# One moving operand of 512 columns, its high half and its low half side by side, in the feed-forward stages and in the expert U loop

## The reference, cut to what matters

```
def peer(xn, w_q, sub_keys, u_tab, v_tab):      # per token: 8 heads x 16 chosen of 16384 experts
    ...
        act = gelu(einsum("phkd,pd->phk", u_tab[ib], tb))
        return einsum("phk,phkd->pd", gb * act, v_tab[ib])

feed-forward, for each of D_FF = 2816 features, 2 layers:
    gate, up = split(x @ w_in)                  # 1024 -> 2 x 2816
    hidden   = silu(causal_conv3(gate) + bias) * up
    y        = hidden @ w_out                   # 2816 -> 1024
```

## Time and profile before

| | |
|---|---|
| median of 3 runs | 1781.97 us |
| the profiled execution's own time | 1776.27 us |
| its span, first to last instruction | 1774.4 us |
| PE (TensorE) busy | 1686.2 us, 95% |
| DVE (VectorE) busy | 1237.4 us, 70% |
| ACT (ScalarE) busy | 902.1 us, 51% |
| granted TensorE clock, mean | 0.978 |
| moved by DMA | 292.43 MB, mean 165 GB/s |

### The profile page before, as it was taken

How to read it: one execution, slowest core, us unless ns; L and a number is a source line. 1 busy time by engine, 2 the same in 40 slices (tenths; PEclk the granted TensorE clock), 3 DMA queues, 4 the chain that set the end, 5 groups by cost and what they waited for, 6 DMA issues and landing times.

```text
span 1774.4 us, 30819 instructions
## 1 busy us (share of the span) xinstructions
PE 1686.2 (95%) x11158; PEld 1543.3 (87%) x11158; DVE 1237.4 (70%) x2305; ACT 902.1 (51%) x1530; POOL 106.6 (6%) x92
## 2 busy tenths in 40 slices
PE   7999799999999999999999998988999989889997
PEld 7999699889999999999988887767999878679997
DVE  7888769979995555555556665666766776466666
ACT  5666632168874444444444454544444445444443
POOL 0000000035540000000000000000000000000000
PEclk9999999999999999999999999989999989889999
DMA  6556634513345555565656665324556544245552
GB/s 206 172 179 215 222 107 149 184 60 109 118 135 198 187 183 187 188 188 183 187 187 193 195 225 180 117 83 143 189 182 187 188 143 130 85 154 180 187 189 96
DMA packets 83290, 292.43 MB, mean 165 GB/s; under 512 B 11152, under 2 KB 12944, under 8 KB 82832
## 3 DMA queue, kind: packets, MB, share of 16 engines
q1 hardware_dynamic: 81568, 286.00, 49.8%
q10 hardware_dynamic: 1648, 5.45, 0.9%
HBM read 289.31 MB, written 2.10 MB: 164 GB/s over the span
## 4 chain that ended last, share of the span: by engine, by line
PE 87%; issue 7%; DVE 3%; ACT 2%; POOL 0%; DMA 0%; SPq 0%; DVEq 0%; ACTq 0%; POOLq 0%
PE ps L1040 16%; PE ps L1041 15%; PE ps L1042 15%; PE ps L1059 10%; PE ps L1061 10%; PE ps L1063 10%; PE ps L1124 5%; PE ps L1148 3%; PE ps L1035 1%; ACT high L670 1%; DVE h_tok L1413 1%; DVE low L1346 1%; DVE xl L1367 0%; DMA subln<-in_subln 0%; PE ps L1112 0%
## 5 line engine op out<-in xcount | busy, mean ns | idle before, releaser
L1346 DVE TENSOR_TENSOR low<-raw,high 128x1024 fp32r<-128x1024 f32 (+1 forms) x517 | 622.3, 1211 | 345.9 <-ACT high L670 332.5
L670 ACT ACTIVATE high<-raw 128x1024 fp32r<-128x1024 f32 (+1 forms) x517 | 540.8, 1048 | 512.2 <-PE ps L1042 283.1
L1040 PE MATMUL ps<-xh,low 128*128 128x256 f32 x2376 | 683.2, 288 | 12.9 <-DVE xl L1367 6.8
L1041 PE MATMUL ps<-xl,high 128*128 128x256 f32 x2376 | 674.8, 284 | 0.0
L1042 PE MATMUL ps<-xh,high 128*128 128x256 f32 x2376 | 674.7, 284 | 0.0
L1040 PEld LDWEIGHTS ps<-xh,low 128*128 128x128 f32 x2376 | 458.1, 193 | 23.1 <-DVE xl L1367 7.5
L1041 PEld LDWEIGHTS ps<-xl,high 128*128 128x128 f32 x2376 | 458.4, 193 | 6.0 <-issue 1.7
L1042 PEld LDWEIGHTS ps<-xh,high 128*128 128x128 f32 x2376 | 458.0, 193 | 0.0
L1059 PE MATMUL ps<-high,yl 128*128 128x512 f32 x688 | 213.7, 392 | 0.1
L1061 PE MATMUL ps<-low,yh 128*128 128x512 f32 x688 | 212.7, 390 | 0.0
L1063 PE MATMUL ps<-high,yh 128*128 128x512 f32 x688 | 212.3, 390 | 0.0
(11 more groups left out here) (243 smaller groups left out, 1495.9 us busy)
## 6 DMA issues: line engine op xcount, KB each, us to landing
raw<-in_v_tab SPq DMA_DIRECT2D x128, 512.0 KB, 3.5
raw<-in_u_tab SPq DMA_DIRECT2D x104, 512.0 KB, 3.5
raw<-in_ffn_in SPq DMA_DIRECT2D x88, 512.0 KB, 3.5
raw<-in_w_mix SPq DMA_DIRECT2D x56, 512.0 KB, 4.2
raw<-in_ffn_out SPq DMA_DIRECT2D x44, 512.0 KB, 3.5
arena<-in_u_tab SPq DMA_DIRECT2D x24, 512.0 KB, 3.6
raw<-in_w_query SPq DMA_DIRECT2D x16, 512.0 KB, 5.7
raw<-in_diff_qk SPq DMA_DIRECT2D x16, 512.0 KB, 3.6
```

Source lines behind the costliest of these rows:

```text
L670: a.activation(cols(high, p, 0, n), cols(raw, p, 0, n), ACT.Copy).then_inc(slot_high[p.slot], 1)
L1040: pe.matmul(dst, left[1], right[0], start=start, stop=False)
L1041: pe.matmul(dst, left[0], right[1], start=False, stop=False)
L1346: v.tensor_tensor(cols(low, p, 0, n), cols(raw, p, 0, n), cols(high, p, 0, n).bitcast(F32), ALU.subtract).then_inc(slot_low[p.slot], 1)
```

## The change

`xh` and `xl` become the two halves of one tensor, `x_parts`. A new `project_in_halves` replaces `project_in` for the expert U pieces of the U loop and for gate and up. Per 128 x 128 block it issues one matmul with the high weights and 512 moving columns (the high chunk and the low chunk) and one with the low weights and 256 columns. The bank then holds two partial results, which have to be added. In the U loop VectorE adds them (`sum_halves`, a `tensor_reduce`) into `u_sum`, and GELU reads that. In the feed-forward stages ScalarE copies one half out of PSUM and VectorE adds the other to it.

```diff
+            def project_in_halves(p, b):
+                pe.wait_ge(slot_low[p.slot], p.count)
+                both = x_parts[:, :].rearrange("p (h k t) -> p h k t", h=2, k=KC)
+                for k in range(KC):
+                    pe.matmul(bank(b).rearrange("p (h t) -> p h t", h=2), cols(high, p, k * PARTS, PARTS), both[:, :, k, :],
+                              start=(k == 0), stop=False)
+                    ins = pe.matmul(bank(b, 0, SEQ), cols(low, p, k * PARTS, PARTS), chunk_of(xh, k), start=False, stop=(k == KC - 1))
+                ins.then_inc(slot_done[p.slot], 1)
# ScalarE, U loop
             def gelu_block(j, it=0, first=False):
-                p = piece_u(j, it)
-                a.wait_ge(slot_done[p.slot], p.count)
+                a.wait_ge(u_summed, it * 4 + (j + 1))
                 if not first:
                     a.wait_ge(coef_low, it * 4 + (j - 1))
-                a.activation(coef[j % 2], bank(4 + j % 4, 0, SEQ), ACT.Gelu_apprx_tanh).then_inc(gelu_ready, 1)
+                a.activation(coef[j % 2], u_sum[j % 2], ACT.Gelu_apprx_tanh).then_inc(gelu_ready, 1)
# TensorE, U loop: the bank is free once it is summed
-                        pe.wait_ge(gelu_ready, it * 4 + j)
-                    project_in(piece_u(j + 3, it), bank(4 + (j + 3) % 4, 0, SEQ))
+                        pe.wait_ge(u_summed, it * 4 + j)
+                    project_in_halves(piece_u(j + 3, it), 4 + (j + 3) % 4)
# VectorE, U loop (halves(b) is the bank as p t h)
+            def sum_halves(j, it=0, first=False):
+                p = piece_u(j, it)
+                v.wait_ge(slot_done[p.slot], p.count)
+                if not first:
+                    v.wait_ge(gelu_ready, it * 4 + (j - 1))
+                v.tensor_reduce(u_sum[j % 2], halves(4 + j % 4), AX.X, ALU.add).then_inc(u_summed, 1)
             def expert_step(j, it):
                 if j + 2 < LATE:
-                    weigh(j + 2, it)
+                    sum_halves(j + 2, it)
                 if j < LATE - 2:
                     ahead(piece_v(j, it))
+                if j + 2 < LATE:
+                    weigh(j + 2, it)
                 if j + 2 < NKEYS:
                     coef_low_part(j + 2, it)
...
# ScalarE, feed-forward
                 def hidden(n, it=0, first=False):
+                    e = n % 2
+                    a.wait_ge(slot_done[piece_gate(l, n, it).slot], piece_gate(l, n, it).count)
+                    a.activation(gate_sum[e], bank(4 + 2 * e, SEQ, SEQ), ACT.Copy).then_inc(s["gate_half"], 1)
                     ahead(piece_gate(l, n, it))
                     a.wait_ge(s["conv_ready"], it * 4 + (n + 1))
                     a.activation(act[n % 2], conv[n % 2], ACT.Silu).then_inc(s["silu_ready"], 1)
+                    a.wait_ge(slot_done[piece_up(l, n, it).slot], piece_up(l, n, it).count)
+                    a.activation(up_sum[e], bank(5 + 2 * e, SEQ, SEQ), ACT.Copy).then_inc(s["up_half"], 1)
                     ahead(piece_up(l, n, it))
...
# VectorE, feed-forward
-                    link(v.tensor_copy(p, at(ffn_params, it * 16 + (l * FF_CHUNKS + n) * 4, 4)))
-                    v.wait_ge(slot_done[piece_gate(l, n, it).slot], piece_gate(l, n, it).count)
+                    v.tensor_copy(p, at(ffn_params, it * 16 + (l * FF_CHUNKS + n) * 4, 4))
+                    v.wait_ge(s["gate_half"], it * 4 + (n + 1))
+                    link(v.tensor_tensor(gate, gate, bank(4 + 2 * e, 0, SEQ), ALU.add))
...
+                    v.wait_ge(s["up_half"], it * 4 + (n + 1))
+                    link(v.tensor_tensor(up, up, bank(5 + 2 * e, 0, SEQ), ALU.add))
                     v.wait_ge(s["silu_ready"], it * 4 + (n + 1))
-                    v.wait_ge(slot_done[piece_up(l, n, it).slot], piece_up(l, n, it).count)
-                    v.tensor_tensor(hid[e], act[e], bank(5 + 2 * e, 0, SEQ), ALU.mult).then_inc(s["hid_ready"], 1)
+                    v.tensor_tensor(hid[e], act[e], up, ALU.mult).then_inc(s["hid_ready"], 1)
```

More of the change, by code:

```diff
@@ L220, in build @@
         h_tok = sb("h_tok", [PARTS, TB * D])
-        xh = sb("xh", [PARTS, KC * SEQ], F32R)
-        xl = sb("xl", [PARTS, KC * SEQ], F32R)
+        x_parts = sb("x_parts", [PARTS, 2 * KC * SEQ], F32R)
+        xh, xl = x_parts[:, 0:KC * SEQ], x_parts[:, KC * SEQ:]
         yh = sb("yh", [PARTS, 2 * SEQ], F32R)
@@ L245, in bank, with halves @@
             return ps[:, b * HALF + lo:b * HALF + lo + n]
+        def halves(b):
+            return bank(b).rearrange("p (h t) -> p t h", h=2)
         def cols(t, p, lo=0, n=D):
@@ L295, in build @@
         coef = [h_tok[:, SEQ * n:SEQ * n + SEQ] for n in range(2)]
+        u_sum = [h_tok[:, 512 + SEQ * n:512 + SEQ * n + SEQ] for n in range(2)]
         weight = spare[:, :]
@@ L359, in build @@
         fpst = [part(1536 + 4 * n, 4) for n in range(2)]
+        gate_sum = [part(1600 + 256 * n, 256) for n in range(2)]
+        up_sum = [part(2112 + 256 * n, 256) for n in range(2)]
         fbias = stats[:, 44:45]
@@ L410, in build @@
         staged_ready, staged_weighed = sem("staged_ready"), sem("staged_weighed")
-        gelu_ready, coef_ready = sem("gelu_ready"), sem("coef_ready")
+        u_summed, gelu_ready, coef_ready = sem("u_summed"), sem("gelu_ready"), sem("coef_ready")
         xf_ready, early_done, early_gelu, early_weighed = (
@@ L426, in build @@
         fz_ready, fexp_ready, bias_ready = (sem(n) for n in ("fz_ready", "fexp_ready", "bias_ready"))
-        ffn_sems = [{n: sem(f"ffn{l}_{n}") for n in ("conv_ready", "silu_ready", "hid_ready", "hid_high", "hid_low")} for l in range(2)]
+        ffn_sems = [{n: sem(f"ffn{l}_{n}") for n in ("gate_half", "up_half", "conv_ready", "silu_ready", "hid_ready", "hid_high", "hid_low")} for l in range(2)]
         block = ctx.enter_context(nc.Block())
@@ L1159, in _ @@
                 pe.wait_ge(staged_weighed, STAGED - LEAD - 3 + j)
-                project_in(piece_u(j), bank(4 + j, 0, SEQ))
+                project_in_halves(piece_u(j), 4 + j)
             def expert_step(j, it):
@@ L1315, in gate_and_up @@
                 def gate_and_up(n, it=0):
-                    project_in(piece_gate(l, n, it), bank(4 + 2 * (n % 2), 0, SEQ))
-                    project_in(piece_up(l, n, it), bank(5 + 2 * (n % 2), 0, SEQ))
+                    project_in_halves(piece_gate(l, n, it), 4 + 2 * (n % 2))
+                    project_in_halves(piece_up(l, n, it), 5 + 2 * (n % 2))
                 def step(n, it):
@@ L1729, in expert_step @@
                     ahead(piece_u(j + 3, it))
+            sum_halves(0, first=True)
+            sum_halves(1, first=True)
             weigh(0)
@@ L1931, in hidden @@
                     e = n % 2
-                    gate = bank(4 + 2 * e, 0, SEQ)
+                    gate, up = gate_sum[e], up_sum[e]
                     p = fpst[e]
-                    link(v.tensor_copy(p, at(ffn_params, it * 16 + (l * FF_CHUNKS + n) * 4, 4)))
-                    v.wait_ge(slot_done[piece_gate(l, n, it).slot], piece_gate(l, n, it).count)
+                    v.tensor_copy(p, at(ffn_params, it * 16 + (l * FF_CHUNKS + n) * 4, 4))
+                    v.wait_ge(s["gate_half"], it * 4 + (n + 1))
+                    link(v.tensor_tensor(gate, gate, bank(4 + 2 * e, 0, SEQ), ALU.add))
                     link(v.tensor_scalar(conv[e], gate, p[:, 2:3], p[:, 3:4], ALU.mult, ALU.add))
@@ L1957, in ffn @@
                 hidden(0)
-                ffn_steps(v, step, chain, 3)
+                ffn_steps(v, step, chain, 4)
             attention("diff", att_sems[0], 3)
```

## The result

The changed kernel takes 1820.99 us (median of 4 runs, 1819.88 to 1824.0), the kernel before 1782.02 us in the same runs. The ratio is 1.022, 95% interval 1.0203 to 1.0238: 39 us slower. The profiled execution took 1821.72 us with a span of 1819.9 us. It stands beside the 1774.4 us span of before.

A forecast was written before the change was run, and what follows sets the result against it. PE was taken to bound the kernel before, and a closed VectorE-ScalarE circle the changed U loop. 45.4 us lost there less 7.3 gained in feed-forward gave 38.1 more: 1814.4 against the profiled execution, 1820 as median, range 1800 to 1840.

The forecast's parts named there:

- The circle: U loop: eight waits between VectorE and ScalarE close on themselves, 6.29 us per step against PE's 5.53; loop 45.4 us longer.
- The one link without a row: U loop, VectorE's sum out of PSUM: taken as 0.684 us, bounds 0.42 and 1.37.
- rival 2: U loop: the reduction is slow on PSUM read with a stride, 1.37 us, total 1865 us; chance 0.07.
- hand-over: U loop, from VectorE's sum to GELU on ScalarE: adds 0.03 us to the reduction, link 0.71.
- PE's pause per step: U loop: PE waits for `coef_low` some 0.75 us in each step once the lead is used up.
- Rival 1: PE's pace decides everywhere, the U-loop circle being under 5.53 us: 13.6 us gained, total 1768 us; chance 0.08.
- Rival 3: U loop: PE's new idle time lowers its granted clock, +78 us, total 1898 us; chance 0.03.
- The feed-forward term: Both feed-forward stages: 88 pieces at 0.092 us save 8.1 us, net of waits 7.3 us.
- the block on TensorE: PE, each 128 x 128 block: 0.359 us falls to 0.346 to 0.349, a saving taken as 0.0115 us.
- waits at the end: Last feed-forward step: PE waits 0.4 us more for the low part of the hidden block, 0.8 for both layers.
- A feed-forward step: Feed-forward stages: PE's step falls from 8.49 to 8.31 us, with PE busy throughout.
- the additions and copies are hidden: Feed-forward stages: PE's 8.31 us step covers VectorE's 6.7 and ScalarE's 4.6 us; uncovered they would cost 72 us.

The follow-up runs named there:

- e1: Changed kernel with one VectorE line moved: in each U-loop step weigh stands ahead of `low` of V, directly behind the sum; 1774.1 us, ratio 0.9959.
- e3: Changed kernel with the U-loop sum taken over 128 of the 256 tokens only, GELU reading these sums twice; 1805.13 us, ratio 1.0129.
- e4: Changed kernel with four more matmuls of 256 columns in each U piece of the U loop; 1821.27 us, ratio 1.0224.
- e6: Changed kernel with the sum of block j+3 placed at the end of VectorE's step j, weigh left behind `low` of V; 1775.64 us, ratio 0.9964.
- e7: e1 with each piece's eight 512-column matmuls first, then its eight of 256, where they alternated; 1764.49 us, ratio 0.9904.

## Why the prediction was right

**The circle.** Its sum, 6.29 us, came out to the hundredth, and the hundredth is luck: GELU of block 2 started at 541.48 and that of block 67 at 950.43, (950.43 - 541.48) / 65 = 6.29. Link by link, against rows 4 to 6, in the step shown above: `high` to `low` 1.07 and 1.08 (forecast 1.09), `low` to the next 1.14 and 1.14, sum to GELU 0.80 (0.71), GELU to `high` V 0.32 (0.33), weigh to `coef_high` 0.45, `coef_high` to `high` U 0.32. The one link without a row, the reduction, took 0.684 us, what the row with as many inputs had the earlier trace rows. Strided reading out of PSUM added nothing, and rival 2 (1.37 us) is out. What I mis-sized is its hand-over, 0.12 us in this step and not 0.03. In the next step the sum starts at 710.71 and GELU at 711.43, 0.72 later, a hand-over of 0.04. Over the 68 steps the two values are about equally common, and GELU comes 6.25 or 6.33 us after the one before it. The mean of this link is 0.755, 0.045 over the forecast; the other seven links together are 5.52 in the step shown, 0.06 under the forecast 5.58. The two errors all but cancel. The loop cost +45.6 between the landmarks, forecast 45.4. PE's pause per step was forecast at 0.76 us; it came to 0.65 to 0.70, since its own step is 5.59 us (as in e1: 705.84 - 700.25) and not 5.53, and inside a longer circle that costs nothing. e1, e3, e4 and e6 show the mechanism itself: reordered it goes, a shorter link shortens it one for one, and more PE work does nothing to the time.

**Rival 1** (PE's pace decides) had its turning point at 5.53 us of circle. It did not come true here. But in e1 and e6, whose circles are below that, PE's pace decides. The gain that this rival named, 13.6 us, is not reached there: the medians lie 8 and 5 us under those of before. e7, with the same matmuls in another order, gains 16.

**Rival 3** (the clock) is out: the granted clock stayed 1.00 in the loop with PE busy 185 of 200 us.

**The feed-forward term was mis-sized.** The step that failed is the block on TensorE: 0.347 us, put together from a spacing of 512 columns among 512s and of 256 among 256s. The rows of the changed kernel give, over ten blocks:

```profile
1281.16 0.39 PE L1068 MATMUL ps<-x_parts,high 128*128 128x512 f32 x1
...
1284.68 0.40 PE L1068 MATMUL ps<-x_parts,high 128*128 128x512 f32 x1
```

3.52 / 10 = 0.352, a saving of 0.007 us per block and not 0.0115, or 0.054 us per piece. Over 88 pieces that is 4.8 us; the landmarks give 4.9, the forecast was 8.1 less 0.8 of waits at the end, 7.3. Those waits were smaller too: in the last step of the first layer the starts of PE's rows on either side of the wait lie 0.89 us apart (1462.13 and 1463.02) where they lay 0.68 apart (1413.23 and 1413.91), 0.2 more and not 0.4, and in the second layer there is no such gap in either kernel. A feed-forward step was to take 8.31 us and takes 8.38:

```profile
1692.32 0.39 ACT L998 ACTIVATE arena<-ps 128x256 f32<-128x256 f32 x1 [1.69 <-PE ps L1070]
...
1700.70 0.39 ACT L998 ACTIVATE arena<-ps 128x256 f32<-128x256 f32 x1 [1.75 <-PE ps L1070]
```

e7 shows that the forecast 0.347 is there to be had, in another order. In the second feed-forward stage the first and the last start of the convolution lay 175.7 us apart before (L1936, 1580.2 to 1755.9); it is 173.2 in the changed kernel (L1969, 1629.0 to 1802.2) and 171.8 in e7 (L1969, 1574.5 to 1746.3). That is 3.9 us less per stage in e7, close to half of the forecast 8.1. In e1 the alternation took nearly all of the gain in the U loop: from first to last GELU 371.1 us (533.7 to 904.8) against 372.0 before (528.8 to 900.8). Part of it is that there the V piece also took 2.78 us instead of 2.75 (703.03 - 700.25). In e7 it takes 2.75 again (705.91 - 703.16), and the same stretch takes 365.9 us (533.4 to 899.3). Why the V piece is slower in the U loop of e1 is open. Its alternating neighbours alone don't do it: in the feed-forward stage of the changed kernel, between the same alternating matmuls, an out piece takes 1697.69 - 1694.95 = 2.74 us.

**That the additions and copies are hidden** in the feed-forward stages held: PE busy 150 of 150 us, VectorE 116.90 / 150 x 8.38 = 6.5 us per step (forecast 6.7).

The mis-sized gain is 2.4 us. With it put right, the forecast would have been 1822.4. That the measured time, 1821.0, lies only 1 us from the forecast 1820 is in part luck, within the scatter of the runs.

## What to carry to other kernels

When two engines work through fixed orders and hand work to each other, write down the circle that the orders close and add it up from start to start. A busy share of 61% says nothing about it, and moving one line can be worth more than the change that it was moved for. Work that hangs on the other engine's last result belongs beside that engine's long instruction, not behind it. Where matmuls of two widths alternate, try them in groups of equal width, and take a spacing for a forecast only from rows in the same company.

## What the runs showed that I had not expected

- Matmuls of 512 and 256 columns with a weight load each cost 0.345 to 0.348 us per pair in groups and 0.351 to 0.353 alternating; over 156 pieces and the V pieces between them the grouped order was 10 us faster.
- A `tensor_scalar` of 256 columns took 0.54 us from PSUM before and 0.41 us from SBUF after the change, which pays part of the added addition back. GELU went the other way, 0.37 us from PSUM and 0.42 from SBUF.
